# The last gate matrix of each layer, loaded by thirteen transfers of spaced rows instead of one

## The chip, the core and the metric

The kernel runs on one core of one Trainium2 chip. The metric is the device time of one execution in microseconds (us), lower is better. The core has five engines with their own instruction streams: TensorE (PE in the profile; its weight loads are PEld), VectorE (DVE), ScalarE (ACT), GpSimd (POOL) and SyncE (SP). Data comes from HBM by DMA: an instruction on SP, ACT or POOL hands a transfer to the core's 16 DMA engines, and a semaphore tells when it has landed. The profile lists issuing instructions as SPq, ACTq or POOLq.

## The reference

It is a two-layer encoder trunk on 256 tokens of width 1024 in float32. Each layer has a mixer (neighbourhood attention beside a Fourier mix in layer 0, a bidirectional mLSTM in layer 1) and then a mixture of 32 experts with two experts for each token. The change is in how the weights of the last expert arrive; what is computed with them is:

```python
def block_fn(args):
    rows, e = args
    xb = x_pad[rows]
    h = jax.nn.silu(xb @ w_gate[e]) * (xb @ w_up[e])
    return h @ w_down[e]
...
for layer in range(DEPTH):
    ...
    x = x + hier_moe(rms_norm(x, moe_norm[layer]), ...)
```

The three matrices of an expert are 1024 by 512 (gate), 1024 by 512 (up) and 512 by 1024 (down), 2 MB each.

## The kernel before

Four stages follow one another: A (mixer of layer 0), B (its experts), C (mixer of layer 1), D (its experts). The expert stages read all 32 experts' weights, 96 pieces of 2 MB, and fill most of the time.

SBUF has eleven weight slots of 16 KB in each of the 128 partitions. SP issues every weight load in one fixed order, one transfer for each piece: `load` (L437 to L441) copies 128 rows of 16 KB, row p of the matrix (viewed as 128 rows of 4096 floats) to partition p of the slot. Piece n uses ring slot n % 11, and before SP issues it, SP waits on `used[ph]` until TensorE has finished the piece that was in the slot. The semaphores `landed_0` to `landed_10` count the arrivals in each slot; `total` and `arrived` (L211 to L222) work out ahead of time which count means "piece n is there". A transfer adds 16 to its slot's semaphore when it has landed.

Piece n is gate, up or down of an expert (n % 3 = 0, 1, 2). The last expert of a stage has pieces 93 (gate), 94 (up) and 95 (down), the constant `PIECES` being 96. `expert_piece` already treats piece 95 apart: it comes in two halves of 1 MB (L449, L450), the first announced by `s_hd`, so that TensorE can begin on it.

TensorE (`moe`, all matmuls at L1311) takes an expert in this order: wait for gate and up, multiply both together (64 matmuls), add the previous expert's result to the sum (`combine`, L1449, 16 matmuls), transpose the routing weights (L1441), wait for ScalarE and VectorE to make h, wait for down, multiply (32 matmuls). For the last expert (index `STATIC - 1`, in `APART`) gate and up are taken one by one, so that gate is used while up is still on its way: gate (64 matmuls of 128 columns), `combine`, transposes, wait for up, up (64 matmuls), `keep_going` (three matmuls of 512 columns whose result nobody uses, L1311 with psum<-cst), down (32), `combine`, the copies of the sums, and in layer 1 the stores of the output.

After stage B, SP goes straight on with the eight 2 MB weight loads of stage C (L499), which queue behind piece 95.

Where 64 rows only are written: the twelve small loads `mem<-in_ev_rel_bias` at the start, issued by GpSimd, go to partitions 0 to 63 (six) and 64 to 127 (six), in runs of 256 bytes. The two loads `g_rows` on ACT's queue have eight rows each of 512 bytes.

Of the kernel before, what the change touches and what calls it, by code (L numbers as in the profile page):

```python
# [30 lines left out]
DC = D // P  # L31
# [23 lines left out]
SLOTS = 11  # L55
SLOT = 4096
PIECES = 3 * EXPERTS
LOOP_AT = EXPERTS // 2
STATIC = EXPERTS - 1
APART = (0, STATIC - 1)  # L60
# [73 lines left out]
def build(nc, a, out):  # L134
    ctx = ExitStack()
    with ctx:
# [21 lines left out]
        def slot(n):  # L158
            return mem[:, PLACE[n] * SLOT:(PLACE[n] + 1) * SLOT]
# [50 lines left out]
        RING = {"B": tuple(range(SLOTS)), "D": (0, 4, 1, 2, 3, 9, 6, 10, 5, 7, 8)}  # L210
# [4 lines left out]
        total, arrived = [0] * SLOTS, {}  # L215
        for ph, n_loads in (("A", n_a), ("B", PIECES), ("C", n_c), ("D", PIECES)):
            for j in range(n_loads):
                if ph in RING and j // 3 == LOOP_AT:
                    continue
                n = DENSE[ph][j] if ph in DENSE else RING[ph][j % SLOTS]  # L220
                total[n] += 16
                arrived[ph, j] = (landed[n], total[n])  # L222

        def dense_slot(ph, j):
# [2 lines left out]
        def piece_slot(ph, n):  # L227
            return slot(RING[ph][n % SLOTS])

        def place(e):  # L230

            return e if e < LOOP_AT else e + 1

# [185 lines left out]
        def _(sp):  # L419
# [17 lines left out]
            def load(l, kind, e, to):  # L437

                name, rows = (("moe_w_gate", DC), ("moe_w_up", DC), ("moe_w_down", DN_ROWS))[kind]
                return sp.dma_start(to.rearrange("p (e f) -> p e f", e=1),  # L440
                                    a[name][l, bass.ds(e, 1)].rearrange("e (p r) f -> p e (r f)", r=rows))  # L441

            def expert_piece(ph, l, n):

                p, kind = divmod(n, 3)
                if n == PIECES - 1:
                    rows = a["moe_w_down"][l, p - 1].rearrange("(p r) f -> p r f", r=DN_ROWS)
                    to, half = piece_slot(ph, n).rearrange("p (r f) -> p r f", r=DN_ROWS), DN_ROWS // 2
                    sp.dma_start(to[:, 0:half], rows[:, 0:half]).then_inc(s_hd, 16)  # L449
                    sp.dma_start(to[:, half:DN_ROWS], rows[:, half:DN_ROWS]).then_inc(arrived[ph, n][0], 16)  # L450
                    return
                load(l, kind, p if p < LOOP_AT else p - 1, piece_slot(ph, n)).then_inc(arrived[ph, n][0], 16)

            def last_and_more(ph, l):

                s = ms[l]
                n0 = 3 * LOOP_AT
                sp.wait_ge(used[ph], n0 + 3 - SLOTS)
# [9 lines left out]

            for n in range(PIECES):
                if n // 3 == LOOP_AT:  # L470
                    if n % 3 == 0:
                        last_and_more("B", 0)
                    continue
                if n < 4:
                    sp.wait_ge(used["A"], n + 1)
                elif n == 4:
                    sp.wait_ge(s_qms, 1)
                elif n == 5:
                    sp.wait_ge(s_sc, HP)
                    sp.wait_ge(s_f2, 2)  # L480
                elif n < 8:
                    sp.wait_ge(s_o, HP)
                elif n < 10:
                    sp.wait_ge(s_proj["A"], 2 if n == 8 else 4)
                elif n == 10:
                    sp.wait_ge(s_proj["A"], 4)
                else:
                    sp.wait_ge(used["B"], n - SLOTS + 1)
                expert_piece("B", 0, n)


            for j in range(n_c):
                if j < 6:
                    sp.wait_ge(used["B"], PIECES - SLOTS + 1 + j)
                elif j == 6:
                    sp.wait_ge(used["B"], PIECES)
                else:
# [3 lines left out]

            for n in range(PIECES):
                if n // 3 == LOOP_AT:
                    if n % 3 == 0:
                        last_and_more("D", 1)
                    continue
                if n == 0:
                    sp.wait_ge(used["C"], 4)
                elif n == 1:
                    sp.wait_ge(s_qTp["C"], 4)  # L510
                    sp.wait_ge(s_dl, HEADS)
                elif n < 4:
                    sp.wait_ge(used["C"], n + 3)
                elif n == 4:
                    sp.wait_ge(s_st, HEADS // 2)
                elif n == 5:
                    sp.wait_ge(s_nu, HEADS // 2)
                elif n == 6:
                    sp.wait_ge(s_nu, HEADS)
                    sp.wait_ge(s_hb, 2 * HEADS)  # L520
                elif n == 7:
                    sp.wait_ge(s_nu, HEADS)
                elif n == 8:
                    sp.wait_ge(s_hn, 2 * HEADS)
                    sp.wait_ge(s_hTp, HEADS)
                elif n < 11:
                    sp.wait_ge(s_proj["C"], 2 if n == 9 else 4)
                else:
                    sp.wait_ge(used["D"], n - SLOTS + 1)
                expert_piece("D", 1, n)  # L530
# [1319 lines left out]
```

## Time and profile before

| what | value |
|---|---|
| median of 3 runs | 1161.43 us (1161.13 to 1163.29) |
| the profiled execution's own time | 1162.22 us |
| its span, first to last instruction | 1160.4 us |
| PE busy / DVE / ACT / POOL | 879.7 / 237.3 / 169.1 / 41.5 us |
| DMA | 439.26 MB, mean 379 GB/s; 425 to 430 GB/s in the expert stages |
| granted TensorE clock, mean | 0.88 |

The profiled execution is 0.8 us above the median, and 1.8 us of its time lie outside the span. PE's share of the span is high because TensorE works at whatever pace the data comes in; in the expert stages the DMA share is 0.99 and more, so one has to look at what the waits end on, not at the busy shares. A share slightly above 1.00 in a short window comes from packets counted where they begin.

### The profile page before, as it was taken

The numbers are of one execution on the slowest core, as the hardware profiler recorded it, in microseconds if no ns is written. First come the engines' busy times: TensorE is split into PE (matmuls) and PEld (weight loads), VectorE is DVE, ScalarE is ACT, GpSimd is POOL, SyncE is SP. The second block draws the span as 40 slices with busy tenths as digits, with TensorE's granted clock in tenths as the row PEclk, the third lists the DMA queues.
The fourth block names the chain that finished last, engine by engine and source line by source line (L and its number), as shares of the span: only waits on it lengthen the run. The fifth ranks groups of instructions, "written<-read, shape, count | busy, mean of one in ns | idle before, by whom it ended". The sixth has DMA issues, their size and how long they took to land.

```text
span 1160.4 us, 20228 instructions
## 1 busy us (share of the span) xinstructions
PE 879.7 (76%) x9135; PEld 510.6 (44%) x9135; DVE 237.3 (20%) x784; ACT 169.1 (15%) x459; POOL 41.5 (4%) x46
## 2 busy tenths in 40 slices
PE   9999995666576757566899999987575676666666
PEld 4454663434344434343544556644242443433343
DVE  2351421111012111110234435211110111111111
ACT  1141310101011101000224232211010110101011
POOL 1651000000000000000000000000000000000000
PEclk9999998879888887888999998988787787878789
DMA  9992999999999999999973258999999999999996
GB/s 347 336 324 99 380 428 425 429 425 429 426 428 426 426 429 424 429 426 425 393 292 118 100 227 353 383 424 429 426 428 426 426 428 425 430 425 427 426 426 271
DMA packets 46261, 439.26 MB, mean 379 GB/s; under 512 B 4640, under 2 KB 5888, under 8 KB 21344
## 3 DMA queue, kind: packets, MB, share of 16 engines
q1 hardware_dynamic: 43632, 433.96, 89.7%
q0 software_dynamic: 1088, 2.97, 1.1%
q8 instruction: 72, 1.18, 0.4%
q10 hardware_dynamic: 1456, 1.04, 0.3%
q14 instruction: 13, 0.11, 0.0%
HBM read 436.91 MB, written 1.05 MB: 377 GB/s over the span
## 4 chain that ended last, share of the span: by engine, by line
PE 48%; DMA 45%; another core or an unknown queue 2%; DVE 2%; ACT 1%; issue 1%; SPq 0%; POOL 0%; DVEq 0%
DMA mem<-in_moe_w_up 44%; PE psum L1311 43%; PE psum L1449 3%; PE psum L1441 1%; PE psum L1332 1%; DMA mem<-in_ev_w_in 1%; SPq L440 0%; DVE mem L962 0%; PE psum L1318 0%; ACT mem L645 0%; DVE mem L1112 0%; DVE mem L1108 0%; PE psum L1610 0%; PE psum L1376 0%
## 5 line engine op out<-in xcount | busy, mean ns | idle before, releaser
L1311 PE MATMUL psum<-mem 128*32 128x256 f32 (+3 forms) x7114 | 671.7, 438 | 258.8 <-DMA mem<-in_moe_w_up 226.2
L1311 PEld LDWEIGHTS psum<-mem 128*32 128x32 f32 (+2 forms) x7114 | 346.8, 132 | 554.9 <-issue 459.9
L1011 DVE TENSOR_TENSOR mem<-psum,mem 128x128 f32<-128x128 f32 x62 | 18.1, 291 | 645.6 <-ACT mem L659 645.6
L659 ACT ACTIVATE mem<-psum 128x128 f32<-128x128 f32 x62 | 17.2, 277 | 522.2 <-PE psum L1311 522.2
L1311 PE MATMUL psum<-mem,x 128*128 128x128 f32 (+1 forms) x576 | 71.5, 285 | 7.2 <-DVE mem L962 3.7
L1449 PE MATMUL psum<-mem 32*128 32x256 f32 x1024 | 73.3, 400 | 3.0 <-ACT mem L665 2.0
L1311 PEld LDWEIGHTS psum<-mem,x 128*128 128x128 f32 x576 | 69.5, 201 | 10.4 <-DVE mem L962 4.5
L1449 PEld LDWEIGHTS psum<-mem 32*128 32x128 f32 x1024 | 46.2, 184 | 30.7 <-issue 23.5
L970 DVE TENSOR_SCALAR mem<-cst,mem 128x128 f32<-128x128 f32 x124 | 37.2, 342 | 20.7 <-PE psum L1441 20.6
L665 ACT COPY mem<-psum 128x256 f32<-128x256 f32 x62 | 23.1, 372 | 95.2 <-PE psum L1311 95.2
L661 ACT COPY mem<-psum 128x256 f32<-128x256 f32 x62 | 23.1, 372 | 64.0 <-PE psum L1441 63.9
L1441 PE MATMUL psum<-cst,mem 128*128 128x128 f32 x128 | 28.5, 305 | 3.2 <-ACT mem L645 3.2
L635 ACT ACTIVATE mem<-psum,g_dealt 128x128 f32<-128x128 f32 x64 | 18.2, 367 | 65.2 <-PE psum L1311 65.2
L1012 DVE STREAM_TRANSPOSE mem<-mem 128x128 f32<-128x128 f32 x62 | 25.1, 405 | 2.1
L962 DVE TENSOR_SCALAR mem<-cst,mem,small 128x32 f32<-128x32 f32 x108 | 23.5, 294 | 7.4 <-PE psum L1449 7.4
L1441 PEld LDWEIGHTS psum<-cst,mem 128*128 128x128 f32 x128 | 13.0, 142 | 24.0 <-issue 20.5
L977 DVE TENSOR_SCALAR mem<-psum,g_dealt 128x128 f32<-128x128 f32 x64 | 18.0, 345 | 18.0 <-PE psum L1311 18.0
L586 POOL DMA_DIRECT2D mem<-in_c_layer x1 | 0.6, 598 | 465.8 <-PE psum L1311 465.8
L582 POOL TENSOR_SCALAR mem<-mem 128x256 f32<-128x256 f32 x16 | 14.5, 921 | 19.6 <-DVE mem L1118 19.6
L1235 DVE SCALAR_TENSOR_TENSOR mem<-psum,mem 128x256 f32<-128x256 f32 (+1 forms) x32 | 11.1, 411 | 3.8 <-PE psum L1311 2.9
L1073 DVE TENSOR_SCALAR mem<-psum,small 128x512 f32<-128x512 f32 x4 | 3.0, 751 | 41.6 <-PE psum L1311 41.6
L1311 PE MATMUL psum<-x,cst 128*128 128x512 f32 x12 | 11.0, 1068 | 0.0
(168 smaller groups left out, 313.8 us busy)
## 6 DMA issues: line engine op xcount, KB each, us to landing
mem<-in_moe_w_gate SPq DMA_DIRECT2D x64, 2048.0 KB, 47.3
mem<-in_moe_w_up SPq DMA_DIRECT2D x64, 2048.0 KB, 48.0
mem<-in_moe_w_down SPq DMA_DIRECT2D x62, 2048.0 KB, 42.8
mem<-in_od_w_in SPq DMA_DIRECT2D x6, 2048.0 KB, 22.5
mem<-in_ev_w_in SPq DMA_DIRECT2D x3, 2048.0 KB, 19.4
mem<-in_ev_w_out SPq DMA_DIRECT2D x2, 2048.0 KB, 28.6
mem<-in_moe_w_down SPq DMA_DIRECT2D x4, 1024.0 KB, 41.9
mem<-in_od_w_out SPq DMA_DIRECT2D x2, 2048.0 KB, 20.0
```

The source lines that it names most:

```text
L635: nc.scalar.activation(xT_m[:, c], bank(6)[:, c * P:(c + 1) * P], ACT.Copy, scale=g_moe[l][:, c:c + 1]).then_inc(s["xT_a"], 1)
L659: nc.scalar.activation(M["sg"], bank(4)[:, 0:P], ACT.Silu).then_inc(s["silu"], 1)
L661: nc.scalar.copy(M["GT"], bank(6)[:, 0:T]).then_inc(s["gtc"], 1)
L665: nc.scalar.copy(M["y"], bank(5)[:, 0:COLS]).then_inc(s["y"], 1)
L962: ins = V.tensor_scalar(Ss_m[:, t, k], slotid[:, 0:CAP], rk3[:, t, e:e + 1], inv_rms(t), ALU.is_equal, ALU.mult)
L970: V.tensor_scalar(Gs_m[:, t], slotid[:, 0:CAP].unsqueeze(1).broadcast_to([P, QUAD, CAP]), rk3[:, t, e:e + 1], G3[:, t, e:e + 1], ALU.is_eq ...
L977: V.tensor_scalar(xT_m[:, c], bank(7)[:, c % 4 * P:(c % 4 + 1) * P], g_moe[l][:, c:c + 1], None, ALU.mult).then_inc(s["xT_v"], 1)
L1011: link(V.tensor_tensor(M["h"], src, M["sg"], ALU.mult))
L1012: V.transpose(hT_m, h_m).then_inc(done, 1)
L1311: return nc.tensor.matmul(out_, lhsT, rhs, start=start, stop=stop)
L1441: last = nc.tensor.transpose(bank(6)[:, t * P:(t + 1) * P], M["Gs"][:, t * P:(t + 1) * P], ident)
L1449: last = nc.tensor.matmul(bank(g)[:, t * COLS:(t + 1) * COLS], M["GT"][g * CAP:(g + 1) * CAP, t * P:(t + 1) * P], M["y"][g * CAP:(g + 1) * ...
```

## The change

Piece 93, the gate matrix of the last expert of each layer, is no longer one transfer of 128 rows. It becomes thirteen transfers, issued by SP one after the other: ten of eight rows that lie sixteen apart (first rows 0 to 4 and 8 to 12) and three of sixteen rows that lie eight apart (first rows 5, 6 and 7). Together they are the same 128 rows of 16 KB into the same partitions. Each adds 16 to the slot's semaphore, so the count that TensorE waits for grows by 12 x 16.

```diff
+UNEVEN = PIECES - 3
+SPACED = tuple((c, 16) for c in range(16) if c % 8 < 5) + tuple((c, 8) for c in range(5, 8))
...
                 n = DENSE[ph][j] if ph in DENSE else RING[ph][j % SLOTS]
-                total[n] += 16
+                total[n] += 16 * (len(SPACED) if ph in RING and j == UNEVEN else 1)
                 arrived[ph, j] = (landed[n], total[n])
...
             def expert_piece(ph, l, n):

                 p, kind = divmod(n, 3)
+                if n == UNEVEN:
+                    rows = a["moe_w_gate"][l, p - 1].rearrange("(p r) f -> p (r f)", r=DC)
+                    for first, step in SPACED:
+                        sp.dma_start(piece_slot(ph, n)[first::step], rows[first::step]).then_inc(arrived[ph, n][0], 16)
+                    return
```

SP's stream at the end of stage D, before the change; `used_D` is the semaphore on which SP waits for a free slot, and 128x4096 is rows by floats in a row:

```order
L440 DMA mem<-in_moe_w_down 128x4096 [waits used_D]
L440 DMA mem<-in_moe_w_gate 128x4096 [waits used_D]
L440 DMA mem<-in_moe_w_up 128x4096 [waits used_D]
L449 DMA mem<-in_moe_w_down 128x2048 [waits used_D]
L450 DMA mem<-in_moe_w_down 128x2048
L535 DMA out<-x 128x2x256 [waits final_v_1] x2
```

The same place after the change:

```order
L442 DMA mem<-in_moe_w_down 128x4096 [waits used_D]
L451 DMA mem<-in_moe_w_gate 8x4096 [waits used_D]
L451 DMA mem<-in_moe_w_gate 8x4096 x9
L451 DMA mem<-in_moe_w_gate 16x4096 x3
L442 DMA mem<-in_moe_w_up 128x4096 [waits used_D]
L456 DMA mem<-in_moe_w_down 128x2048 [waits used_D]
L457 DMA mem<-in_moe_w_down 128x2048
L542 DMA out<-x 128x2x256 [waits final_v_1] x2
```

One row has become thirteen transfers, all behind the same wait; up and down keep their places behind them. Line numbers are two to seven higher because of the added lines. The same happens at the end of stage B, where the loads of stage C follow. No other engine's stream has a different order.

## Rows read from the trace of the kernel before

**Rows 1.** Page, parts 1 and 2: busy time by engine; the span in 40 slices.

```profile
span 1160.4 us, 20228 instructions
...
PE 879.7 (76%) x9135; PEld 510.6 (44%) x9135; DVE 237.3 (20%) x784; ACT 169.1 (15%) x459; POOL 41.5 (4%) x46
...
PEclk9999998879888887888999998988787787878789
DMA  9992999999999999999973258999999999999996
GB/s 347 336 324 99 380 428 425 429 425 429 426 428 426 426 429 424 429 426 425 393 292 118 100 227 353 383 424 429 426 428 426 426 428 425 430 425 427 426 426 271
```

**Rows 2.** Page, part 4: chain that ended last, by engine and by line.

```profile
PE 48%; DMA 45%; another core or an unknown queue 2%; DVE 2%; ACT 1%; issue 1%; SPq 0%; POOL 0%; DVEq 0%
DMA mem<-in_moe_w_up 44%; PE psum L1311 43%; PE psum L1449 3%; PE psum L1441 1%; PE psum L1332 1%; DMA mem<-in_ev_w_in 1%; SPq L440 0%; DVE mem L962 0%; PE psum L1318 0%; ACT mem L645 0%; DVE mem L1112 0%; DVE mem L1108 0%; PE psum L1610 0%; PE psum L1376 0%
```

**Rows 3.** PE alone, end of layer 1's expert stage: start, us, what, idle before, releaser.

```profile
1117.56 3.66 PE L1311 MATMUL psum<-mem 128*32 128x256 f32 x64 [1.69 <-issue]
...
1132.26 5.05 PE L1311 MATMUL psum<-mem 128*32 128x256 f32 x64 [7.74 <-DMA mem<-in_moe_w_up]
...
1138.69 1.93 PE L1311 MATMUL psum<-mem 128*32 128x256 f32 x32
1141.96 1.95 PE L1311 MATMUL psum<-mem 128*32 128x128 f32 x64 [1.33 <-DMA mem<-in_moe_w_gate]
1143.84 1.15 PE L1449 MATMUL psum<-mem 32*128 32x256 f32 x16
...
1146.84 1.95 PE L1311 MATMUL psum<-mem 128*32 128x128 f32 x64 [1.48 <-DMA mem<-in_moe_w_up]
1148.72 2.84 PE L1311 MATMUL psum<-cst 128*128 128x512 f32 x6
1151.49 1.93 PE L1311 MATMUL psum<-mem 128*32 128x256 f32 x32
1153.92 1.15 PE L1449 MATMUL psum<-mem 32*128 32x256 f32 x16 [0.49 <-ACT mem L665]
```

**Rows 4.** Windows at that end, columns as their first line says.

```profile
core 0: us, PE busy (x) PEld busy (x) DVE busy (x) ACT busy (x) POOL busy (x), PEclk, DMA share, GB/s
1085.00:1135.00 50.00, 32.52 (x402) 19.52 (x406) 5.03 (x16) 4.20 (x13) 0.00 (x0) 0.80 1.01 427
1140.00:1144.00 4.00, 2.67 (x80) 1.98 (x76) 0.00 (x0) 0.37 (x1) 0.00 (x0) 1.00 1.03 428
1144.00:1145.00 1.00, 1.00 (x17) 0.65 (x18) 0.00 (x0) 0.00 (x0) 0.00 (x0) 1.00 0.70 295
1145.00:1146.00 1.00, 0.35 (x2) 0.12 (x2) 0.00 (x0) 0.00 (x0) 0.00 (x0) 1.00 0.54 229
1146.00:1149.00 3.00, 2.17 (x65) 1.97 (x66) 0.00 (x0) 0.14 (x1) 0.00 (x0) 1.00 0.53 218
1149.00:1150.00 1.00, 1.00 (x3) 0.39 (x3) 0.70 (x2) 0.40 (x2) 0.00 (x0) 1.00 0.37 156
1150.00:1151.00 1.00, 1.00 (x4) 0.38 (x2) 0.00 (x0) 0.00 (x0) 0.00 (x0) 1.00 0.24 98
1151.00:1152.00 1.00, 1.00 (x14) 0.34 (x16) 0.00 (x0) 0.00 (x0) 0.00 (x0) 1.00 0.00 0
```

**Rows 5.** PE alone, end of layer 0's expert stage.

```profile
550.25 1.95 PE L1311 MATMUL psum<-mem 128*32 128x128 f32 x64 [0.75 <-DMA mem<-in_moe_w_gate]
...
555.18 1.95 PE L1311 MATMUL psum<-mem 128*32 128x128 f32 x64 [1.54 <-DMA mem<-in_moe_w_up]
557.07 2.84 PE L1311 MATMUL psum<-cst 128*128 128x512 f32 x6
559.84 1.93 PE L1311 MATMUL psum<-mem 128*32 128x256 f32 x32
...
567.69 2.73 PE L1311 MATMUL psum<-mem 128*128 128x512 f32 x5
```

**Rows 6.** Transfers of 727 to 1151 us: packets by size, then by queue.

```profile
DMA packets 12418, 178.80 MB, mean 422 GB/s; under 512 B 1375, under 2 KB 1375, under 8 KB 1375
...
q1 hardware_dynamic: 12383, 178.26, 99.1%
q8 instruction: 31, 0.51, 0.5%
```

**Rows 7.** The same for 1.70 to 1.95 us, an eight-row transfer on ACT's queue q10.

```profile
DMA packets 64, 0.03 MB, mean 115 GB/s; under 512 B 8, under 2 KB 64, under 8 KB 64
...
q10 hardware_dynamic: 16, 0.00, 7.0%
```

**Rows 8.** SP and ACT issuing transfers, timeline: start, us, what.

```profile
0.74 0.62 ACTq L591 DMA_DIRECT2D g_rows<-in_ev_norm  x1
...
1.40 0.30 ACTq L592 DMA_DIRECT2D g_rows<-in_od_h_gain  x1
...
1094.87 0.33 SPq L440 DMA_DIRECT2D mem<-in_moe_w_down  x1
1095.24 3.28 SPq L440 DMA_DIRECT2D mem<-in_moe_w_gate  x1
1098.57 4.23 SPq L440 DMA_DIRECT2D mem<-in_moe_w_up  x1
1109.04 0.33 SPq L449 DMA_DIRECT2D mem<-in_moe_w_down  x1
1109.41 1.95 SPq L450 DMA_DIRECT2D mem<-in_moe_w_down  x1
```

**Rows 9.** Windows: full rows alone, with 64-partition transfers beside them, and later.

```profile
20.00:30.00 10.00, 10.00 (x25) 4.40 (x24) 0.75 (x1) 0.69 (x1) 0.00 (x0) 1.00 1.05 393
36.00:46.00 10.00, 10.00 (x25) 4.50 (x24) 5.93 (x6) 2.83 (x3) 2.60 (x4) 1.00 1.04 224
50.00:60.00 10.00, 10.00 (x36) 5.31 (x35) 3.38 (x5) 0.69 (x1) 10.00 (x8) 1.00 1.06 427
```

**Rows 10.** Transfers of 36 to 46 us: by queue, and the 64-partition issues.

```profile
q0 software_dynamic: 474, 1.29, 64.4%
q1 hardware_dynamic: 472, 0.95, 40.0%
...
mem<-in_ev_rel_bias POOLq DMA_DIRECT2D x4, 128.0 KB, 9.8
```

## The prediction, made before the changed kernel ran

> **What bounds the kernel now.** I read the page first: DMA moves 425 to 430 GB/s through both expert stages, and only layer changes and the last slice fall off [rows 1]. The chain of waits agrees: 44% of the span stands under the landing of a moe_w_up piece, 43% under the expert matmuls, which share that time by turns [rows 2]. In the expert stages the bound is the stream of weights, so a change in how the last pieces arrive can only act at the end of each stage, where nothing is left to buffer.
>
> So I read TensorE at the end of stage D [rows 3]. It stood idle 1.33 us for the last gate (used from 1141.96), 1.48 us for the last up (from 1146.84), and from there it is a fixed chain: up 1.9, keep_going until 1151.5, down, result. The two halves of the last down are not what it waits for: keep_going ends as they arrive. The end of the kernel therefore moves with the landing of **up**. Layer 0 has the same picture, with the gate used from 550.25 and up from 555.18 [rows 5].
>
> Then the windows there [rows 4]. The DMA share is 1.03 until 1144, then 0.70, 0.54, 0.53 for three microseconds, 0.37, 0.24, and nothing after 1151. Half of the 16 engines have run out by about 1144 to 1146.4, the other half work on to 1149 to 1151.0. A transfer counts as landed only with its slowest part, so every late piece waits for the slower eight. The area after 1144 is 0.70 + 0.54 + 3 x 0.53 + 0.37 + 0.24 = 3.4 us: shared out evenly, all would end at 1147.4. That is the room for an uneven gate matrix: at most 3.6 us in layer 1. In layer 0 the loads of stage C follow and hide the tail from the windows; I take it to be like layer 1's, as its waits are.
>
> **The change part by part.** A 128-row transfer uses all 16 engines: 1375 small packets for the 86 transfers from 727 to 1151 us are 16 for each, one from each engine [rows 6]. An eight-row transfer of before leaves 16 packets on q10, eight of data and eight small ones [rows 7]: eight engines, one row each. So the ten transfers of eight rows give one row each to eight engines, if it is always the same eight, and the three of sixteen give one row to each of the 16. Eight engines get 13 rows, eight get 3, in place of 8 and 8.
>
> A row costs, at 427 GB/s over 16 engines [rows 4], 16384 B / 26.7 GB/s = 0.61 us. Five rows are 3.1 us. **If rows still cost 0.61 us** and the 13 go to the early eight, these end at 1146.4 + 3.1 = 1149.5 and the late ones at 1151.0 - 3.1 = 1147.9; the last end moves by 1.5 to 1.8 us, say -1.7 a layer. TensorE can follow: it is free for the gate 1.33 us earlier, and gate, combine and transposes need 3.4 us before up [rows 3].
>
> **But where do the rows go?** The trace has one place in which full rate and many engines meet few partitions: from 36 to 46 us, when GpSimd's transfers into 64 of the 128 partitions ran beside the weights. All engines were busy (share 1.04), yet only 224 GB/s moved, against 393 before and 427 after [rows 9]; the 64-partition transfers took 64% of engine time for 1.29 MB [rows 10]. Either their 256-byte runs are to blame, or a group of partitions takes data at one engine's pace, and engines that write to the same group share it. The second reading bounds the change: in a full transfer each engine has its own partitions, while eight rows sixteen apart, and four such transfers in a row with neighbouring first rows, need not be spread like that.
>
> The bounds for a layer, by that reading. Lower: a row costs 427/224 = 1.9 times 0.61 us. 13 x 0.61 x 1.9 = 15.2 us in place of 8 x 0.61 = 4.9, so the early eight end at 1146.4 + 10.3 = 1156.7, which is 5.5 us after the 1151.1 of before. Upper: the late eight, still writing ordinary rows, join in, and three share for the ten transfers: 10 x 1.84 + 3 x 1.17 = 21.9 us, an end at 1163.4, +12.3. The late ones are there for part of the time and only on some of the partitions, so I take the middle, **+8.9**. Below nothing: the -1.7 above.
>
> The Trainium skill has this as a rule. "SBUF — State Buffer", section "Door 1: The DMA port swizzle", says that DMA writes go through 16 ports picked by bits 2 to 4 and bit 6 of the partition number; by it eight rows sixteen apart reach four ports, two engines on each, where a full transfer gives every engine its own. "DMA: Bandwidth & Descriptors", section "Why a DMA increments its semaphore by 16 and not by 1", says that such a transfer runs on the lowest-numbered engines; no row here shows which eight those are. The trace agrees with the first as far as 224 against 427 GB/s can show; without the rule the sum is -1.7 a layer.
>
> **The clock.** PEclk averages 0.80 over the waits of the last experts [rows 4]. After an idle 7.7 us, 64 matmuls took 5.05 us where 3.66 is the full-speed time [rows 3]. A later gate means about 10 us of idle TensorE, so the gate part starts at the lower level. Up follows 4.9 us later, and TensorE's 3.4 us of work before it become 4.8 with the same 1.4 us added: between 0 and, if all of it ran at half speed, 2 us. I take +0.5.
>
> **SP.** Thirteen issues in place of one, with up and both halves of down queued behind them on SP. Single issues took 0.33 us at best, eight-row ones on ACT 0.62 and 0.30, one behind another up to 3.28 [rows 8]. 13 x 0.4 = 5 us, ended near 1101, 40 us before the gate is used: hidden by the queue of eleven slots. The upper bound is a rival.
>
> **Sum.** +8.9 + 0.5 = +9.4 a layer, twice: +18.8. Layer 0's shift passes on whole, as the C loads lie behind it in the same queues and TensorE goes on at 567.7 [rows 5]. Span 1160.4 + 18.8 = 1179.2, plus the 1.8 us outside it 1181.0, less the 0.8 us by which this execution is above the median: **1180.2 us**. Its own range is 1161.4 + 2 x 5.5 = 1172.4 to 1161.4 + 2 x 14.3 = 1190.
>
> **The rivals.**
>
> 1. *Rows cost the same wherever they land, and the early eight get 13.* -1.7 a layer, **1158.0 us**. For it: in steady state the 16 engines move 26.7 GB/s each, which may be the engine's own limit, and the 256-byte runs explain the 224 GB/s as well. Against it: the factor is so near two. It decides from the point at which a spaced row costs over 0.61 + 4.7/13 = 0.97 us: then the early eight pass 1151.1 and the gain is a loss.
>
> 2. *The same, but the 13 rows go to the late eight.* 1151.1 + 3.1: +3.1 a layer, **1167.6 us**. Nothing in the rows says which eight carry a small transfer. 31 instruction fetches fell in stage D [rows 6]; if they all use the same eight engines, these would be the late ones, but not whether that is the eight of a small transfer.
>
> 3. *SP becomes the bound.* At 3.28 us an issue [rows 8], thirteen take 43 us from 1095.2, to 1138; up would be issued at 1138 to 1142 and land some 7 us later, near 1149, 2 us after the 1146.8 of before: +2 a layer, **1165.4 us**. Against it: 3.28 us is the time of a 128-row transfer behind another, not of eight rows.
>
> 4. *The change doesn't shift anything*: the small transfers take different eights in turn, and the rows stay balanced and apart. **1161.4 us**.
>
> **How the numbers follow.** Sharing 0.64, rival 1 0.21, rival 2 0.05, rival 3 0.04, rival 4 0.06. A measurement of this kernel can tell about 0.2%, 2.3 us, from no change. Slower: 0.64 + 0.05 + 0.04 = 0.73; faster: rival 1 without its weakest outcomes, 0.20; the same: 0.07. The range must reach to rival 1, since the likeliest case holds only 0.64: 1157 to 1188.
>
> **What would show it.** Sharing: at the end of stage D the DMA share falls to about a half or below before the last gate is used and stays there for 10 us or more, the first wait of the last expert grows from 1.33 to about 10 us with DMA moe_w_gate as releaser, and gate and up then come 4.9 us apart as before. Rival 1: the share stays near 1.0 to 1147 and falls within 3 us, and up's matmuls start near 1145.1. Rival 2: the half-share stretch grows from 5 to 11 us at full rate for those that work. Rival 3: SP's small issues take over 3 us each and up is issued after 1135. The prediction is wrong if the wait for the gate grows by less than 4 us; it is right for the wrong reason if layer 0 doesn't move while layer 1 does.

## The result, and the profile after

The changed kernel takes **1196.23 us** (median of 4 runs, 1193.91 to 1196.68), the kernel before 1162.36 us beside it (4 runs, 1161.13 to 1164.37). The ratio is 1.0288, with a 95% interval of 1.0273 to 1.0302: 34 us slower, where 19 were forecast, and 8 us above the end of the range. The profiled execution took 1196.32 us, its span is 1194.5 us.

The page of the changed kernel: the 40 slices, and the chain of work that ended last.

```profile
span 1194.5 us, 20252 instructions
...
PEclk9999897878888878786999998988788788877887
DMA  9973899999999999999973257999999999999994
GB/s 348 344 286 140 368 426 427 428 427 426 426 427 426 428 426 427 425 427 245 368 264 131 97 236 321 426 427 427 427 427 426 427 425 428 426 427 426 428 305 159
...
DMA 49%; PE 43%; another core or an unknown queue 3%; SPq 2%; DVE 1%; issue 1%; ACT 1%; POOL 0%; DVEq 0%
DMA mem<-in_moe_w_up 40%; PE psum L1318 38%; DMA mem<-in_moe_w_gate 4%; DMA mem<-in_moe_w_down 4%; PE psum L1456 2%; SPq L451 1%; PE psum L1448 1%; DMA mem<-in_ev_w_in 1%; SPq L442 0%; PE psum L1339 0%; PE psum L1325 0%; DVE mem L1119 0%; DVE mem L1115 0%; PE psum L1617 0%
```

Against [rows 1] the middle of both expert stages is untouched (425 to 428 GB/s). Two places are new: the slice with 245 GB/s, where layer 0's experts end, and the last two with 305 and 159. The row above the 245 still reads 9: **the engines are as busy as before and move little more than half**. In the chain, gate and down, which [rows 2] doesn't name, have 4% each.

TensorE alone at the end of layer 0's experts, then of layer 1's. Columns: start, us, what, idle before and its releaser. L1311 of before is now L1318, L1449 is L1456.

```profile
568.84 3.64 PE L1318 MATMUL psum<-mem 128*32 128x128 f32 x64 [12.64 <-DMA mem<-in_moe_w_gate]
...
585.55 4.96 PE L1318 MATMUL psum<-mem 128*128 128x512 f32 x11
```

```profile
1150.85 6.41 PE L1318 MATMUL psum<-mem 128*32 128x256 f32 x64 [9.29 <-DMA mem<-in_moe_w_up]
...
1160.39 1.93 PE L1318 MATMUL psum<-mem 128*32 128x256 f32 x32 [1.69 <-DMA mem<-in_moe_w_down]
1175.16 3.64 PE L1318 MATMUL psum<-mem 128*32 128x128 f32 x64 [12.84 <-DMA mem<-in_moe_w_gate]
1178.73 1.92 PE L1456 MATMUL psum<-mem 32*128 32x256 f32 x16
...
1180.95 1.96 PE L1318 MATMUL psum<-mem 128*32 128x128 f32 x64
```

The wait for the last gate grew from 1.33 us [rows 3] to 12.84, in layer 0 from 0.75 [rows 5] to 12.64. The piece before it waited too, 1.69 us for a down matrix that was issued *ahead* of the spaced rows and has the ordinary shape. Stage C's first matmuls moved from 567.69 [rows 5] to 585.55: layer 0 costs 17.9 us. The last up moved from 1146.84 to 1180.95, 34.1 us, so layer 1 adds 16.2.

Windows at the end of layer 1, with the columns of [rows 4], and one in layer 0.

```profile
1085.00:1135.00 50.00, 31.58 (x382) 18.66 (x386) 6.27 (x22) 4.20 (x13) 0.00 (x0) 0.76 1.01 427
...
1144.00:1148.00 4.00, 0.00 (x0) 0.00 (x0) 0.00 (x0) 0.00 (x0) 0.00 (x0) 0.78 1.08 414
1148.00:1159.00 11.00, 7.86 (x82) 4.17 (x82) 0.95 (x3) 0.54 (x2) 0.00 (x0) 0.62 1.02 217
1159.00:1170.00 11.00, 1.93 (x32) 1.13 (x32) 0.34 (x2) 0.48 (x2) 0.00 (x0) 0.85 0.99 217
1170.00:1176.00 6.00, 0.84 (x16) 0.79 (x20) 0.00 (x0) 0.00 (x0) 0.00 (x0) 0.50 0.81 320
1176.00:1180.00 4.00, 4.00 (x68) 3.29 (x61) 0.00 (x0) 0.00 (x0) 0.00 (x0) 0.50 0.22 92
1180.00:1184.00 4.00, 4.00 (x77) 2.67 (x74) 0.68 (x2) 0.54 (x2) 0.00 (x0) 0.95 0.10 41
```

```profile
540.00:564.00 24.00, 9.65 (x114) 5.25 (x114) 1.30 (x4) 1.02 (x3) 0.00 (x0) 0.71 1.01 215
```

Read these as a balance. From 1148 to 1170 all engines are busy and 217 GB/s move: 22 us do the work of 22 x 217 / 427 = 11.2 us, a loss of **10.8 us**. The rest is 6 x 320 / 427 + 4 x 92 / 427 + 4 x 41 / 427 = 5.7 us of full rate, spread over 14. In sum 16.9 us of full rate lie behind the start of the crowding. Shifted back by layer 0's 17.9 us, that start is 1130.1 in the kernel before, where 13.9 us of full rate and the 3.4 us of [rows 4] follow: 17.3, the same bytes to within 0.4 us. There all ended at 1151.1, here at 1184 - 17.9 = 1166.1. So the transfers of layer 1 end 15.0 us later: 10.8 in the crowded stretch and 4.2 in a tail in which few engines still work (shares 0.22 and 0.10 are 3.5 and 1.6 engines of 16).

TensorE adds 1.2 us: its gate took 3.64 us in place of 1.95 and the combine 1.92 in place of 1.15, at a granted clock of 0.50 (the 1.2 GHz level) after 12.84 us idle. By the semaphore events, which no row here shows, up was complete at 1179.7, and its matmuls start at 1180.95 with no wait noted. 15.0 + 1.2 = 16.2.

All eight late engines, those that finish a matrix some 5 us behind the others, were slow in that stretch, on rows of the ordinary shape too: by the semaphore events their eight rows of the down matrix ahead of the spaced rows took 9.3 to 9.8 us, where eight rows took 4.9 in the kernel before.

SP issuing the last gate and up, timeline.

```profile
1111.00 14.98 SPq L451 DMA_DIRECT2D mem<-in_moe_w_gate  x13
1126.03 1.16 SPq L442 DMA_DIRECT2D mem<-in_moe_w_up  x1
```

The thirteen took 15 us to issue, 1.15 each, not the 0.4 of the forecast. Up was still issued at 1126, long before the crowding began.

### The profile page after: what moved, and what is told of

Its sections match the earlier page's. It is cut to its first block, busy times and chain, and to the rows that moved or that the text cites. A ratio compares the mean times of both kernels' runs of the same rounds, so it can differ in the third digit from the quotient of the medians.

```text
span 1194.5 us, 20252 instructions
## 1 busy us (share of the span) xinstructions
PE 888.4 (74%) x9135; PEld 517.9 (43%) x9135; DVE 237.4 (20%) x784; ACT 169.1 (14%) x459; POOL 41.5 (3%) x46
## 3 DMA queue, kind: packets, MB, share of 16 engines
q10 hardware_dynamic: 1456, 1.04, 0.3%
## 4 chain that ended last, share of the span: by engine, by line
DMA 49%; PE 43%; another core or an unknown queue 3%; SPq 2%; DVE 1%; issue 1%; ACT 1%; POOL 0%; DVEq 0%
DMA mem<-in_moe_w_up 40%; PE psum L1318 38%; DMA mem<-in_moe_w_gate 4%; DMA mem<-in_moe_w_down 4%; PE psum L1456 2%; SPq L451 1%; PE psum L1448 1%; DMA mem<-in_ev_w_in 1%; SPq L442 0%; PE psum L1339 0%; PE psum L1325 0%; DVE mem L1119 0%; DVE mem L1115 0%; PE psum L1617 0%
## 5 line engine op out<-in xcount | busy, mean ns | idle before, releaser
L1318 PE MATMUL psum<-mem 128*32 128x256 f32 (+3 forms) x7114 | 678.4, 443 | 284.2 <-DMA mem<-in_moe_w_up 227.3
L1318 PEld LDWEIGHTS psum<-mem 128*32 128x32 f32 (+2 forms) x7114 | 352.2, 134 | 580.8 <-issue 468.0
L1318 PE MATMUL psum<-mem,x 128*128 128x128 f32 (+1 forms) x576 | 74.3, 292 | 7.2 <-DVE mem L969 3.7
L1318 PEld LDWEIGHTS psum<-mem,x 128*128 128x128 f32 x576 | 72.2, 208 | 10.4 <-DVE mem L969 4.5
L1456 PE MATMUL psum<-mem 32*128 32x256 f32 x1024 | 74.3, 404 | 2.9 <-ACT mem L672 2.0
L1456 PEld LDWEIGHTS psum<-mem 32*128 32x128 f32 x1024 | 46.9, 187 | 31.1 <-issue 23.8
L1318 PE MATMUL psum<-x,cst 128*128 128x512 f32 x12 | 11.0, 1066 | 0.0
```

What stands on the lines that cost most here:

```text
L1318: return nc.tensor.matmul(out_, lhsT, rhs, start=start, stop=stop)
L1456: last = nc.tensor.matmul(bank(g)[:, t * COLS:(t + 1) * COLS], M["GT"][g * CAP:(g + 1) * CAP, t * P:(t + 1) * P], M["y"][g * CAP:(g + 1) * ...
```

## The experiments

**The question.** The mechanism was in the text beforehand, the size was not: a layer's end moved by more than my upper bound. Theory P (places): the loss is where rows land in SBUF. Its rivals: H, rows 256 KB apart in HBM are slow to read; E, eight engines can't do more; N, thirteen transfers cost more than one; and U, a sum of the uneven share, 13 rows against 3.

### 1. The spacings alone

A kernel without the encoder, which loads whole weight matrices (16 KB rows into 128 partitions) by one pattern after another, each waited for before the next. The core of it:

```python
for e in range(pieces):
    for to, of in cuts:          # rows in SBUF, rows in HBM
        sp.dma_start(slot[e][to], w[e][of]).then_inc(landed[i], 16)
```

> This kernel leaves the whole encoder out: it only loads 16 KB weight rows from HBM into four SBUF slots, in fourteen patterns one after the other, each alone and to its end, and copies x to the output. In order, with 8 MB each unless said: (0) 128 rows in one transfer; (1) eight rows sixteen apart; (2) eight rows four apart; (3) eight neighbouring rows, 4 MB; (4) sixteen rows eight apart; (5) sixteen neighbouring rows, 4 MB; (6) source rows sixteen apart, destination four apart; (7) source four apart, destination sixteen apart; (8) source sixteen apart, destination neighbouring; (9) 64 neighbouring rows, 4 MB; (10) every second row, 4 MB; (11) as 0; (12) one whole piece, one piece as the changed kernel cuts it, two whole pieces, all queued together; (13) the same with eight rows four apart in place of sixteen. Theory P (a group of destination partitions takes data at one engine's pace, 26.7 GB/s): (1) 107 GB/s, (2) 213, (3) 53, (4) 213, (5) 107, (6) as 2, (7) as 1, (8) as 3, (9) 213, (10) 427, (12) over 10 us longer than (13). Rival H (rows 256 KB apart in HBM collide): (1), (6) and (8) slow, (2), (3) and (7) at 213. Rival E (only the number of engines counts): every eight-row pattern 213, every sixteen-row one 427, (12) equal to (13). The group sizes of theory P come from the Trainium skill, SBUF State Buffer, Door 1: The DMA port swizzle.

Windows inside the patterns, in this order: whole; eight rows 16 apart; eight 4 apart; eight neighbours; sixteen rows 8 apart; sixteen neighbours; source 16 and destination 4 apart; source 4 and destination 16 apart; source neighbours and destination 16 apart; and then, in the mix of the changed kernel (whole matrix, the thirteen, two whole ones), the crowded stretch and its slowest part. The last three columns are granted clock, DMA share, GB/s.

```profile
8.00:26.00 18.00, 0.00 (x0) 1.00 1.01 431
31.00:103.00 72.00, 0.00 (x0) 1.00 0.50 113
107.00:150.00 43.00, 0.00 (x0) 1.00 0.49 190
155.00:218.00 63.00, 0.00 (x0) 1.00 0.50 62
223.00:258.00 35.00, 0.00 (x0) 1.00 1.00 213
263.00:296.00 33.00, 0.00 (x0) 1.00 0.97 115
300.00:342.00 42.00, 0.00 (x0) 1.00 0.50 192
346.00:418.00 72.00, 0.00 (x0) 1.00 0.50 113
425.00:500.00 75.00, 0.00 (x0) 1.00 0.50 107
```

```profile
566.00:584.00 18.00, 0.00 (x0) 1.00 0.98 180
570.00:578.00 8.00, 0.00 (x0) 1.00 0.96 141
```

A share of 0.50 means eight engines. With rows four apart they move 190 GB/s, near eight times 26.7; sixteen apart 113, near four times. The pair in which source and destination differ settles it: **the rate follows the destination** (192 with destination four apart, 113 with destination sixteen apart), whatever the source. H and E are out. The Trainium skill's "SBUF — State Buffer", section "Door 1: The DMA port swizzle", gives sixteen ports, picked by bits 2 to 4 and bit 6 of the partition; by it eight rows reach four ports when sixteen apart, eight when four apart, two when neighbours. The rows agree: 113, 190 and 62 GB/s. (A "group" of partitions, here and below, is the partitions of one such port.)

The ninth row is not the pattern that the expectation names. A cut is the pair (destination, source), and the kernel has `zip(spaced(16, 8), spaced(1, 8))`: neighbouring rows of HBM, put sixteen apart in SBUF. So its 107 belongs beside the two 113, and it is a third case of the rate following the destination. The opposite, read sixteen apart and written as neighbours, was not run.

The last two windows are the changed kernel's transfers without any TensorE: all sixteen engines busy, 180 GB/s for 18 us, and 141 for 8 us of them. One expectation was missed: the mix with rows sixteen apart was to take over 10 us longer than the one with rows four apart. By the semaphore events they took 35.8 and 28.0 us, a difference of 7.8. So rows four apart are not free either, as experiment 3 shows in the kernel.

### 2. HBM distance taken out of the kernel

```diff
+                    at = 0
                     for first, step in SPACED:
+                        count = P // step
-                        sp.dma_start(piece_slot(ph, n)[first::step], rows[first::step]).then_inc(arrived[ph, n][0], 16)
+                        sp.dma_start(piece_slot(ph, n)[first::step], rows[at:at + count]).then_inc(arrived[ph, n][0], 16)
+                        at += count
```

> The changed kernel, but the thirteen transfers take neighbouring rows of the gate matrix in HBM and put them into the same spaced partitions; the last expert of each layer is therefore computed with rows of its gate matrix in the wrong places. Theory P (the destination decides): as the changed kernel, 1194 to 1197 us. Rival H (the distance in HBM decides): near 1158 to 1165 us.

1195.83 us, ratio 1.0294 (1.0257 to 1.033), the same loss. The layout in HBM plays no part that these runs can show. "DMA: Bandwidth & Descriptors" of the Trainium skill, section "Latency and other measured facts", tells of row pitches of 512 KiB and more that slow copies between HBM tensors down; at the 256 KB here no run shows such a cost.

### 3. Four apart, and sixteen rows to a transfer

```diff
-SPACED = tuple((c, 16) for c in range(16) if c % 8 < 5) + tuple((c, 8) for c in range(5, 8))
+SPACED = tuple((c, 4, 8) for c in (0, 1, 2, 3, 32, 33, 34, 35, 64, 96)) + tuple((c, 4, 16) for c in (65, 66, 67))
```

(first row, step, count.) The engines' shares stay 13 and 3. Each eight-row transfer now reaches eight groups of partitions, one for each of its engines. The three of sixteen rows do not: rows 65, 69 and on to 125 all lie in partitions 64 to 127, eight groups for sixteen engines.

> The changed kernel with the same counts, ten transfers of eight rows and three of sixteen, but rows four apart in place of sixteen and eight. Theory P: the eight engines of a small transfer write to eight different groups, so the large loss goes; five rows of each of these engines still go to groups that another engine writes to, so no gain is sure: 1158 to 1168 us. Rival E (thirteen transfers or eight engines are the cost, wherever rows lie): as the changed kernel, 1194 to 1197 us.

1182.1 us, ratio 1.0175 (1.0141 to 1.021): **a miss**, 14 us above the expected. Windows at the end of layer 1:

```profile
1136.00:1145.00 9.00, 2.48 (x24) 1.36 (x28) 0.00 (x0) 0.00 (x0) 0.00 (x0) 0.68 1.01 428
1146.00:1153.00 7.00, 5.26 (x86) 2.81 (x78) 1.30 (x4) 1.02 (x3) 0.00 (x0) 0.99 0.97 210
1153.00:1156.00 3.00, 0.00 (x0) 0.00 (x0) 0.00 (x0) 0.00 (x0) 0.00 (x0) 1.00 1.06 355
1156.00:1162.00 6.00, 0.00 (x0) 0.00 (x0) 0.00 (x0) 0.00 (x0) 0.00 (x0) 0.53 0.83 186
```

While the first eight transfers, into partitions 0 to 63, are written, the rate is full. It halves at about 1146, when the last five come, into 64 to 127. My expectation had asked only whether the engines of *one* transfer keep apart. In the two eight-row transfers the other eight engines were still writing ordinary rows, and 210 GB/s from 16 busy engines is what eight groups take: both halves of the engines aim at partitions 64 to 127. In the three of sixteen rows all sixteen engines aim there anyway, which the expectation overlooked. For the eight-row ones the reading rests on rates here; C of experiment 4 tests it alone.

```diff
-SPACED = tuple((c, 16) for c in range(16) if c % 8 < 5) + tuple((c, 8) for c in range(5, 8))
+SPACED = tuple((c, 8) for c in range(8))
```

> The last gate matrix as eight transfers of sixteen rows eight apart: every engine keeps its eight rows, so nothing is shifted between engines, but two engines meet in a group of partitions. Theory P: a piece takes 9.4 us in place of 4.9, +4.5 us or more a layer, 1170 to 1176 us. Rival E, and the theory that the uneven load of the engines alone makes the loss: 1161 to 1163 us.

1183.85 us, 1.019 (1.015 to 1.0231): also a miss, by 8 us, with shares of eight rows each for all engines. So U is not the bulk of the loss. Its crowded stretch:

```profile
1141.00:1162.00 21.00, 9.27 (x114) 5.12 (x114) 1.30 (x4) 1.02 (x3) 0.00 (x0) 0.77 1.01 216
```

Eight transfers of sixteen rows alone should take 8 x 16 rows x 16 KB / 213 GB/s = 9.8 us. They hold the rate down for 21 us: the ordinary rows around them are slow as well. That gave theory **G**: a crowded group slows *every* engine, not only those that aim at it.

### 4. Engines that only look on

Again no encoder. Each of six patterns queues three whole matrices, sixteen small transfers and two whole matrices at once, so that the second eight engines, which get nothing of the small ones, go on to the whole matrices behind. A: partitions 0 to 63, four apart; B: the same partitions, eight apart (four groups); C: 64 to 127, four apart; D and E: sixteen apart in two orders; F: 0 to 63, eight neighbours.

> This kernel leaves the encoder out and only loads 16 KB weight rows. Six patterns, each alone: three whole pieces on all 16 engines, then sixteen eight-row transfers (2 MB, on eight engines), then two whole pieces, all queued at once, so that eight engines are in the small transfers while the other eight have gone on to whole pieces. A: destinations in partitions 0 to 63, rows four apart; B: the same half, eight apart; C: partitions 64 to 127, four apart; D: sixteen apart over all; E: as D, in another order of first rows; F: partitions 0 to 63, neighbouring rows. The question is what becomes of the engines that only write whole pieces. Local theory (engines are slowed only where they themselves meet another in a group of partitions): while the small transfers run, A moves 427 GB/s, B about 320 (eight engines at half, eight at full rate), C about 213, F about 270. Global theory (one crowded group slows all engines, those in other groups too): B and F fall to 213 or less, as C does.

Windows while the small transfers are written: A, B, then B when they are done and the first eight engines write their rows of the last two whole matrices, then C, D, F.

```profile
24.00:32.00 8.00, 0.00 (x0) 1.00 1.00 424
60.00:78.00 18.00, 0.00 (x0) 1.00 0.98 215
78.00:87.00 9.00, 0.00 (x0) 1.00 0.48 204
106.00:124.00 18.00, 0.00 (x0) 1.00 0.98 212
152.00:178.00 26.00, 0.00 (x0) 1.00 1.01 153
...
258.00:284.00 26.00, 0.00 (x0) 1.00 1.01 154
```

B decides. Its small transfers keep to partitions 0 to 63 and the other eight engines to 64 to 127, so no group is wanted by both. If only those that collide lost, the onlookers would keep 8 x 26.7 = 214 GB/s beside the 107 of four groups, some 320 in all. All sixteen are busy and move 215 together. The semaphore events agree: each small transfer takes 1.2 us and the onlookers' two whole matrices 19 us, where both took half as long in A. As soon as the small ones are done, at about 78, eight engines alone move 204 GB/s, their full rate. A is the control: the same engines on the same partitions without a collision leave 424. So engines that have their groups to themselves can lose half their rate to crowding elsewhere. F, four engines on each of two groups, gives the same answer: 154 where the local theory has 270.

The Trainium skill names a mechanism of this kind for transfers between cores only: by "DMA: Bandwidth & Descriptors", section "Back-pressure in remote DMA", a saturated destination port clogs the path back to the source engines and to engines sharing it. B fits that picture for loads from HBM; which path is shared here, no run shows.

D falls to 153 GB/s (E, the same rows in another order, to 168, not shown), lower than the 217 of the changed kernel with nearly the same transfers. The mix of experiment 1 falls as low for a while, to 141. Why, I can't say.

### 5. How few engines are enough

Five more patterns, three whole matrices, sixteen tiny transfers, three whole ones. G: two neighbouring rows, so two engines on one group; H: two rows four apart; I: four neighbours; J: four rows four apart; K: four rows sixteen apart.

> No encoder; the output is not the reference's. How much crowding does it take to slow the engines that only write whole pieces? Five patterns, one after the other, each three whole pieces, sixteen small transfers, three whole pieces, queued at once. Small transfers: G two neighbouring rows (two engines, one group of partitions), H two rows four apart (two engines, two groups), I four neighbouring rows (four engines, one group), J four rows four apart (four engines, four groups), K rows 0, 16, 32, 48 and on (four engines, two groups, two engines on each). The three whole pieces ahead take about 15 us at full rate; in the 12 us behind them the engines without small transfers write the whole pieces that follow. A row is 0.61 us of one engine, 26.7 GB/s each. Theory L (only engines that aim at the same group slow one another; the bystanders lose nothing here, and what was seen with eight engines needs many of them): G 14 x 26.7 + 26.7 = 400 GB/s, I 12 x 26.7 + 26.7 = 347, K 12 x 26.7 + 2 x 26.7 = 374. Theory G (a crowded group slows all): G and K near 215 to 260, I below G. H and J are the controls: 420 to 430 by both.

G while its rows 0 to 7 are written and then behind them; H and I during their small transfers; J during its rows 16 to 31, 32 to 47 and 48 to 63.

```profile
24.00:27.00 3.00, 0.00 (x0) 1.00 1.03 393
27.00:39.00 12.00, 0.00 (x0) 1.00 1.02 283
...
78.00:93.00 15.00, 0.00 (x0) 1.00 1.00 226
...
126.00:144.00 18.00, 0.00 (x0) 1.00 1.00 251
...
180.00:183.00 3.00, 0.00 (x0) 1.00 0.99 218
183.00:186.00 3.00, 0.00 (x0) 1.00 1.02 371
186.00:189.00 3.00, 0.00 (x0) 1.00 1.04 218
```

**My controls were none.** H and J should have stayed at 420 to 430 and fell to 226 and, over all of its stretch, 274. I had counted only collisions among the small transfers' own engines. Rows 8 to 31 of H, and rows 16 to 31 and 48 to 63 of J, lie in groups that other engines are writing at that time for the whole matrices. J's windows bear this out: the rate is 218, then 371 while rows 32 to 47 come, then 218 again. So does H, whose rate is still at 431 while its rows 0 to 7 come, and so do A and C of the experiment before.

Read this way H and J are evidence, not controls. In H two groups have two engines each, and twelve engines have their groups to themselves. If only the four lost, 12 x 26.7 + 2 x 26.7 = 374 would be left; 226 are. For J it is 8 x 26.7 + 4 x 26.7 = 320 against 218. K gave 223 (not shown).

G shows the limit. While its rows 0 to 7 are written, its two engines share one group and nobody else wants it. Their rows take 1.2 us by the semaphore events, and the fourteen others write their next whole matrix in 5 us, as ever: 393 GB/s, the 400 of theory L. Only from row 8 on, where by the same reading as for H a third engine wants the group, does the rate fall to 283, against 13 x 26.7 + 26.7 = 374 if only the three lost. **Theory G as I stated it, any crowded group slows all, is thus too wide**: one pair on one group costs the others nothing here, two pairs (H) halve them all. What decides between the two was not tested.

### 6. Number of transfers, one layer, another order

Thirteen transfers of all 128 rows in place of spaced ones, cut by columns:

```diff
-                    for first, step in SPACED:
-                        sp.dma_start(piece_slot(ph, n)[first::step], rows[first::step]).then_inc(arrived[ph, n][0], 16)
+                    for first, end in SPACED:    # twelve of 256 columns, one of 1024
+                        sp.dma_start(piece_slot(ph, n)[:, first:end], rows[:, first:end]).then_inc(arrived[ph, n][0], 16)
```

> The last gate matrix in thirteen transfers, but each over all 128 rows and a part of the columns (1 KB runs, the last 4 KB), so every engine keeps its rows and its partitions. Theory P: the number of transfers costs nothing that is seen, 1160 to 1164 us. Rival (thirteen issues on SP and thirteen completions are the loss): 1180 us or more.

1162.22 us, ratio 0.9999 (0.9988 to 1.0011), and the waits of the last expert are close to those of [rows 3]; below them SP's issues of this run:

```profile
1142.32 1.95 PE L1318 MATMUL psum<-mem 128*32 128x128 f32 x64 [1.54 <-DMA mem<-in_moe_w_gate]
...
1147.24 1.95 PE L1318 MATMUL psum<-mem 128*32 128x128 f32 x64 [1.51 <-DMA mem<-in_moe_w_up]
```

```profile
1093.62 42.09 SPq L451 DMA_DIRECT2D mem<-in_moe_w_gate  x13
1135.75 0.44 SPq L442 DMA_DIRECT2D mem<-in_moe_w_up  x1
```

N is out, and with it any cost of SP's. These thirteen issues took 42 us, nearly three times as long as in the changed kernel, up went out at 1135.75 only, and it was still there in time.

```diff
-                if n == UNEVEN:
+                if n == UNEVEN and ph == "D":
```

> The change in layer 1 alone; layer 0 loads its last gate matrix in one transfer. Both layers lose by the same mechanism: half the loss, 1178 to 1180 us. If layer 0's loss were mostly in the loads of stage C behind it: nearer to 1185 us than to 1178.

1179.36 us, 1.0152 (1.01 to 1.0204), +16.4. The last gate and up of its layer 1:

```profile
1157.05 3.64 PE L1318 MATMUL psum<-mem 128*32 128x128 f32 x64 [12.90 <-DMA mem<-in_moe_w_gate]
...
1162.42 1.96 PE L1318 MATMUL psum<-mem 128*32 128x128 f32 x64
```

Up is 15.6 us behind the 1146.84 of [rows 3], close to the 16.2 by which layer 1 moved up above. The layers add up.

```diff
-SPACED = tuple((c, 16) for c in range(16) if c % 8 < 5) + tuple((c, 8) for c in range(5, 8))
+SPACED = tuple((c, 16) for c in (0, 8, 4, 12, 1, 9, 2, 10, 3, 11)) + tuple((c, 8) for c in range(5, 8))
```

> The changed kernel with the ten eight-row transfers in another order (first rows 0, 8, 4, 12, 1, 9, 2, 10, 3, 11 in place of 0 to 4, 8 to 12), so that neighbours in the queue go to other groups of partitions. If engines meet mainly because four transfers in a row aim at the same groups, the loss falls by a third or more, to 1180 to 1188 us. If two engines meet within each transfer whatever its neighbours are: 1190 to 1197 us.

1191.73 us, 1.0259 (1.0216 to 1.0302). The interval overlaps that of the changed kernel (1.0273 to 1.0302), so a gain isn't shown. Transfers in a row with first rows in different groups help little if at all: the engines meet inside each transfer.

No experiment points to a kernel that beats the one before. Moving the rows of the late eight to the early eight takes rows of partitions 64 to 127, which then meet the late eight there (C: 212 GB/s with all engines busy). The 3.4 us of room in [rows 4] can't be had this way; that is an inference from C and from experiment 3.

## Why the prediction was right in kind and wrong in size

**What bounds the kernel: right.** The end moved with the landing of up in both layers; all that came between were TensorE's 1.2 us.

**Where the rows go: right.** Rows sixteen apart crowd, as the sharing reading had it. The eight that carry them are the early ones: by the semaphore events, which no row here shows, seven of the early eight are through with the piece before at 1147.7 to 1148.8, and seven parts of the first eight-row transfer land at 1149.0 to 1150.1, while no late engine is through with that piece before 1156.8. Rival 2 wanted full rate for those that work, and is refuted by the 217 GB/s.

**Rival 1, rows that cost the same: refuted** by 217 GB/s with a share of 1.0 and by experiment 1. A spaced row costs 16384 B x 8 / 113 GB/s = 1.16 us, above the 0.97 from which I had said that the gain is a loss. **Rival 3: refuted** by experiment 6, where SP took the 42 us that this rival needed and the time stayed the same. **Rival 4: refuted** by the result.

**The step that failed is the price of the sharing, the term +8.9 us.** It measured +15.0 in layer 1, above even the upper bound of +12.3. I wrote: "The late ones are there for part of the time and only on some of the partitions, so I take the middle". Sharing was treated as a matter between engines that want the same group. Experiments 4 and 5 show engines with groups of their own at half rate beside such crowding. In the changed kernel all eight late ones ran at half rate on the ordinary rows that were queued ahead of the spaced ones, and the rate stayed at 217 GB/s for 22 us. That is why a down matrix issued earlier came late (1.69 us) and the wait of the expert before grew from 7.74 [rows 3] to 9.29.

The upper bound had nearly that length, 21.9 us, but this is in part luck. It was thirteen rows of the early eight, most of them at 1.84 us. At 217 GB/s from sixteen engines a row takes 1.2 us, and the 22 us hold 4.8 MB: the 2 MB of spaced rows and more than as much again of ordinary ones, ahead of them and behind. With the upper bound in the sum, +12.3 a layer, the time would have been 1187. The other 2.7 us a layer are in the tail: I let the early eight end together, but thirteen of the sixteen engines were through with up by 1172.3 and the last three at 1175.7, 1177.2 and 1179.7. What spreads them was not tested.

**A sign that failed with it.** For sharing I had said that the DMA share falls to about a half or below before the last gate is used and stays there for 10 us. It stayed at 0.99 and more until 1170 and was 0.81 up to the gate's use at 1175.16. I had the late eight finished and idle while the early ones worked off their rows; in fact they were busy, at half rate. The wait for the gate (12.84 us, forecast about 10) and the 5.8 us from gate to up (forecast 4.9) came about as said. And the range ended at 1188, though the sharing case by itself reached to 1190.

The warning was in the rows: in [rows 9] the share was 1.04 and the rate 224, and by [rows 10] the crowded transfers took 64% of engine time while the ordinary ones, 40% of it, moved 0.95 MB in 10 us. Ordinary packets there should have moved 0.40 x 10 x 427 = 1.7 MB. They were slow by the same factor of 1.8, though not all of them go to the partitions of the transfer beside them; I read only the 64-partition ones.

**The clock: right in kind, too small.** +0.5 forecast, 1.2 measured. Gate and combine ran at the lower level, 1.7 and 0.8 us longer. The 2.5 us are set off against the 1.48 us for which TensorE had waited for up before [rows 3].

**SP:** 5 us forecast, 15 measured, hidden either way.

**Layer 0 passes its shift on whole: right.** Experiment 5 gave half the loss. Sum of what was measured: 17.9 + 15.0 + 1.2 = 34.1 us, against 18.8.

## What to carry to other kernels

Near full DMA rate, ask of every transfer which groups of partitions its engines write at the same moment, and whether other queued transfers' engines write them too; crowded groups can slow loads that have nothing to do with them. A DMA share of 1.0 with half the GB/s of the neighbouring windows is the mark of it. To even out the last transfers, cut them by columns at full height (free here, 0.9999) rather than by rows, and where a price lies between two bounds, first ask who else is slowed.

## What the hardware showed that I had not expected

- Onlookers can lose as much as those that collide: 215 GB/s from sixteen busy engines where eight of them had their groups to themselves, and 226 where twelve had. One pair of engines on one group left the others at full rate (393 in all); why two pairs do not is open.
- Balanced shares don't help: eight transfers of sixteen rows eight apart cost 1.9%.
- Eight-row transfers cost SP 1.15 us each to issue behind a full queue, thirteen full-height ones 42 us in all, and neither cost anything in the end.
- Left open: two patterns of rows sixteen apart fell to 153 and 168 GB/s, and the mix of experiment 1 to 141 for 8 us, where the changed kernel kept 217.
